# A decoder step with a product-key expert layer: row numbers by exclusive-or and minimum, negated scores, sink column and gate sums on ScalarE

## What is computed

```python
def banded_attention(q, k, v, sink):
    ...
    s = jnp.where(mask[None, :, None, None], s, -jnp.inf)
    lse = jax.nn.logsumexp(s, axis=-1)
    if sink is not None:
        lse = jnp.logaddexp(lse, sink.astype(jnp.float32)[:, :, None])
    p = jnp.exp(s - lse[..., None])
...
        s1, i1 = lax.top_k(sc[:, :, 0], PEER_TOPK)
        s2, i2 = lax.top_k(sc[:, :, 1], PEER_TOPK)
        cand = (s1[..., :, None] + s2[..., None, :]).reshape(...)
        cid = (i1[..., :, None] * N_KEYS + i2[..., None, :]).reshape(...)
        top_s, pos = lax.top_k(cand, PEER_TOPK)
        eid = jnp.take_along_axis(cid, pos, axis=-1)
        gate = jax.nn.softmax(top_s, axis=-1)
        act = jax.nn.gelu(jnp.einsum('cd,chkd->chk', hc, u[eid]))
        return jnp.einsum('chk,chkd->cd', gate * act, v[eid])
```

## Time and profile before

| | |
|---|---|
| median of 3 runs | 3233.87 us (3221.91 to 3236.2) |
| span of the profiled execution | 3236.3 us |
| instructions | 37338 |
| granted TensorE clock, mean | 0.946 |
| moved by all transfers | 1258.27 MB, 389 GB/s in the mean |
| of these, the gathers' queue | 1086.39 MB, 83.0% of 16 engines' span |
| the other transfers' main queue | 169.50 MB, 13.9% |

### The profile page before, as it was taken

How to read it: one execution, slowest core, us unless ns; L and a number is a source line. 1 busy time by engine, 2 the same in 40 slices (tenths; PEclk the granted TensorE clock), 3 DMA queues, 4 the chain that set the end, 5 groups by cost and what they waited for, 6 DMA issues and landing times.

```text
span 3236.3 us, 37338 instructions
## 1 busy us (share of the span) xinstructions
PE 2680.4 (83%) x8698; PEld 1435.6 (44%) x8698; DVE 2511.3 (78%) x5990; ACT 1835.9 (57%) x5839; POOL 1352.4 (42%) x1044
## 2 busy tenths in 40 slices
PE   7768878889997888899899888888788888767776
PEld 4444444445553444555444444443334444334342
DVE  1288868888788998878888887887678888977775
ACT  1246645578544556865555567774455556555554
POOL 0043423354343344433433444542344544556663
PEclk9889989999998998989999999998999999999999
DMA  8999989999999999989999999999999999999997
GB/s 329 353 372 413 382 346 420 394 411 419 398 382 381 406 405 394 409 344 395 403 398 358 405 385 379 415 410 349 356 373 397 403 386 399 393 409 421 421 421 317
DMA packets 189061, 1258.27 MB, mean 389 GB/s; under 512 B 24592, under 2 KB 32616, under 8 KB 44432
## 3 DMA queue, kind: packets, MB, share of 16 engines
q0 software_dynamic: 149760, 1086.39, 83.0%
q1 hardware_dynamic: 39080, 169.50, 13.9%
HBM read 1247.04 MB, written 43.37 MB: 399 GB/s over the span
## 4 chain that ended last, share of the span: by engine, by line
DMA 28%; DVE 24%; PE 23%; ACT 7%; issue 7%; DVEq 4%; SPq 3%; POOL 2%; ACTq 1%; POOLq 0%
DMA uv_ring<-in_peer_uv,idx 24%; PE acc L1787 10%; DVE uv_ring L2482 10%; DVE accs L2489 4%; PE pS L1655 3%; PE pS L1528 3%; POOL uv_ring L1469 2%; ACT bent L2086 2%; PE pA L1678 2%; ACT wv L2089 1%; SPq L1366 1%; SPq L1333 1%; ACT diag L1859 1%; DMA S<-in_cache_swa 1%; PE acc L1528 1%
## 5 line engine op out<-in xcount | busy, mean ns | idle before, releaser
L1469 POOL DMA_INDIRECT uv_ring<-in_peer_uv,idx x1024 | 1336.9, 1306 | 1841.8 <-PE acc L1787 1384.3
L1787 PE MATMUL acc<-uv_ring,diag 128*128 128x512 f32 x2536 | 1291.1, 645 | 373.9 <-ACT diag L1859 373.0
L2482 DVE SCALAR_TENSOR_TENSOR uv_ring<-uv_ring,hb 128x1024 f32<-128x1024 f32 x1032 | 1240.1, 1221 | 316.9 <-DMA uv_ring<-in_peer_uv,idx 292.6
L1787 PEld LDWEIGHTS acc<-uv_ring,diag 128*128 128x128 f32 x2536 | 477.5, 201 | 966.6 <-ACT diag L1859 509.0
L2082 ACT ACTIVATE cube<-dots 128x1 f32<-128x1 f32 x1032 | 205.4, 199 | 849.9 <-DVE uv_ring L2482 844.3
L2489 DVE SCALAR_TENSOR_TENSOR accs<-uv_ring,wv,accs 128x1024 f32<-128x1024 f32 x390 | 499.3, 1280 | 28.9 <-ACT wv L2089 28.1
L2086 ACT ACTIVATE bent<-dots,cube 128x1 f32<-128x1 f32 x1032 | 399.1, 387 | 74.6 <-issue 3.5
L1801 PE MATMUL acc<-maskB,zeros 128*96 128x256 f32 x1600 | 394.2, 386 | 0.0
L1801 PEld LDWEIGHTS acc<-maskB,zeros 128*96 128x96 f32 x1600 | 263.8, 167 | 172.2 <-issue 109.5
L1859 ACT ACTIVATE diag<-diag,wv 128x128 f32<-128x128 f32 x634 | 254.6, 402 | 54.3 <-issue 4.0
L2089 ACT ACTIVATE wv<-bent,dots 128x1 f32<-128x1 f32 x634 | 245.3, 387 | 45.1 <-issue 1.4
(11 more groups left out here) (287 smaller groups left out, 2265.5 us busy)
## 6 DMA issues: line engine op xcount, KB each, us to landing
wbuf<-in_w_q SPq DMA_DIRECT2D x40, 1024.0 KB, 9.7
out_dil_s<-in_cache_dil SPq DMA_DIRECT2D x8, 4092.0 KB
wbuf<-in_w_in SPq DMA_DIRECT2D x26, 1024.0 KB, 9.7
wbuf<-in_w_out SPq DMA_DIRECT2D x20, 1024.0 KB, 9.7
uv_ring<-in_peer_uv,idx POOLq DMA_INDIRECT x1024, 10.8
uv_ring<-in_w_in SPq DMA_DIRECT2D x6, 1024.0 KB, 16.7
keysT<-in_keys SPq DMA_DIRECT2D x40, 128.0 KB, 12.4
T<-in_xT_all SPq DMA_DIRECT2D x8, 512.0 KB, 15.4
```

Source lines behind the costliest of these rows:

```text
L1469: pool.indirect_dma_start(uv_ring[:, entry % RING, :], None, peer_uv, bass.IndirectOffsetOnAxis(rows, 0))\
L1787: m = pe.matmul(acc[0:R, side * 512:(side + 1) * 512], w, uv_ring[:, entry % RING, D + side * 512:D + (side + 1) * 512], start=first, stop ...
L2482: dve.scalar_tensor_tensor(row, row, GELU_C, h, ALU.mult, ALU.mult, accum_out=dots[:, e % RING:e % RING + 1]).then_inc(u_dot, 1)
```

## The change

It has five parts.

- Scores are formed with -0.125 and a minimum, so that the reduction gives the negated maximum at once (`anm`). The sinks are negated once. ACT's exponents take scale -1.
- The sink becomes one more column of the banded scores. ACT copies it there ahead of its wait for the maxima, and the exponent's own sum contains it; the addition on DVE goes.
- The place bits and the key numbers are coded such that the exclusive-or of a wanted rank with an entry is the key number where the ranks agree, and 128 or more where not. A minimum over the 16 entries then gives the number. `places_of` becomes one OR and one shift with AND, and comparison and product become one exclusive-or.
- The subtraction before the gates' exponents goes: ACT makes the negated largest sum by a copy and takes it as a bias. It does so one tile at a time, and takes the sums along (`accum_out`).
- `times_of` has new costs for `sm`, `vd`, `r1`, `r2`, `r3`, `gd` and `ge`.

```diff
-        return (("DVE", {"r2": (2.5, 3.36), "r3": (1.77, 2.58), "gd": (0.75, 0.79)}[kind][tiles - 1]),)
+        return (("DVE", {"r2": (1.25, 1.8), "r3": (0.95, 1.5), "gd": (0.5, 0.52)}[kind][tiles - 1]),)
-        "s": (("PE", 0.64 if first else 0.64 + 0.21 * n),), "sm": (("DVE", 1.12 if first else 1.12 + 0.135 * n),),
+        "s": (("PE", 0.64 if first else 0.64 + 0.21 * n),), "sm": (("DVE", 0.88 if first else 0.88 + 0.135 * n),),
-        "vd": (("DVE", 0.5),), "vo": (("ACT", 0.41),),
+        "vd": (("DVE", 0.27),), "vo": (("ACT", 0.41),),
-        "r0": (("DVE", 3.23),), "r1": (("DVE", 2.75),), "ge": (("ACT", 0.15),),
+        "r0": (("DVE", 3.23),), "r1": (("DVE", 2.48),), "ge": (("ACT", 0.9),),
-        "so": (("DVE", 1.15),), "sr0": (("DVE", 3.2),), "sr1": (("DVE", 2.7),), "sr2": (("DVE", 2.55),), "sr3": (("DVE", 1.74),),
-        "sge": (("ACT", 0.15),), "sgd": (("DVE", 1.08),),
+        "so": (("DVE", 1.15),), "sr0": (("DVE", 3.2),), "sr1": (("DVE", 2.7),), "sr2": (("DVE", 1.3),), "sr3": (("DVE", 0.95),),
+        "sge": (("ACT", 0.6),), "sgd": (("DVE", 0.8),),
...
                 b = par if t == 0 or piped(t) else 0
-                act.wait_ge(a_max, A + 1)
                 n = blocks_of(t) * P
                 B = S[:, 640 * par:640 * par + P] if t == 0 else S[:, 0:n]
-                Aw = S[:, 640 * par + 256:640 * par + 384] if t == 0 else S[:, D:D + 256]
-                act.activation(B, B, ACT.Exp, bias=anm[:, b, 0:1], accum_out=aden[:, b, 0:1])
-                act.activation(Aw, Aw, ACT.Exp, bias=anm[:, b, 1:2], accum_out=aden[:, b, 1:2])
-                act.activation(aden[:, b, 2:3], sink[:, h:h + 1], ACT.Exp, bias=anm[:, b, 1:2]).then_inc(a_exp, 1)
+                Aw = S[:, 640 * par + 256:640 * par + 385] if t == 0 else S[:, D:D + 257]
+                if A == 0:
+                    act.wait_ge(a_max, 1)
+                last = 640 * par + 384 if t == 0 else D + 256
+                copy(S[:, last:last + 1], sink[:, h:h + 1])
+                act.drain()
+                act.wait_ge(a_max, A + 1)
+                act.activation(B, B, ACT.Exp, scale=-1.0, bias=anm[:, b, 0:1], accum_out=aden[:, b, 0:1])
+                act.activation(Aw, Aw, ACT.Exp, scale=-1.0, bias=anm[:, b, 1:2], accum_out=aden[:, b, 1:2]).then_inc(a_exp, 1)
 
...
                 n = len(prompt_of(GROUPS[g]))
-                act.activation(gexp[:, 0:n, :], gsub[:, 0:n, :], ACT.Exp).then_inc(r_exp, 1)
+                copy(gneg[:, 0:n], candv[:, 0:n, 0], -1.0)
+                act.drain()
+                for u in range(n):
+                    m = act.activation(gexp[:, u, :], candv[:, u, :], ACT.Exp, bias=gneg[:, u:u + 1],
+                                       accum_out=gsum[:, u:u + 1])
+                m.then_inc(r_exp, 1)
 
             def sample_gate_exp():
                 act.wait_ge(sr_sub, 1)
-                act.activation(gexp[0:64, 1, :], gsub[0:64, 1, :], ACT.Exp).then_inc(sr_exp, 1)
+                copy(gneg[0:64, 1:2], candv[0:64, 1, 0:1], -1.0)
+                act.drain()
+                act.activation(gexp[0:64, 1, :], candv[0:64, 1, :], ACT.Exp, bias=gneg[0:64, 1:2],
+                               accum_out=gsum[0:64, 1:2]).then_inc(sr_exp, 1)
 
...
                     dve.wait_ge(c2_in, 16 * (9 + NS))
+                    dve.tensor_scalar(sink[:, :], sink[:, :], -1.0, None, ALU.mult)
                 dve.wait_ge(a_s, A + 1)
...
                     dve.tensor_tensor_reduce(S[:, base:base + P], pS[:, 512 * par:512 * par + P], maskB[:, 7 * P:],
-                                             0.125, NEG, ALU.add, ALU.max, amax[:, b, 0:1])
+                                             -0.125, -NEG, ALU.add, ALU.min, anm[:, b, 0:1])
                     dve.tensor_tensor_reduce(S[:, base + 256:base + 384], pS[:, 512 * par + 256:512 * par + 384],
-                                             maskA[:, P:], 0.125, NEG, ALU.add, ALU.max, amax[:, b, 1:2])
+                                             maskA[:, P:], -0.125, -NEG, ALU.add, ALU.min, anm[:, b, 1:2])
                 else:
                     need(dve, a_t, A)
                     n = blocks_of(t) * P
-                    dve.tensor_tensor_reduce(S[:, 0:n], pS[:, 0:n], maskB[:, D - n:], 0.125, NEG, ALU.add, ALU.max,
-                                             amax[:, b, 0:1])
+                    dve.tensor_tensor_reduce(S[:, 0:n], pS[:, 0:n], maskB[:, D - n:], -0.125, -NEG, ALU.add, ALU.min,
+                                             anm[:, b, 0:1])
                     near = pS[:, 768:1024] if piped(t) else pM[:, 0:256]
-                    dve.tensor_tensor_reduce(S[:, D:D + 256], near, maskA[:, :], 0.125, NEG,
-                                             ALU.add, ALU.max, amax[:, b, 1:2])
-                D_()
-                dve.tensor_tensor(amax[:, b, 1:2], amax[:, b, 1:2], sink[:, h:h + 1], ALU.max)
-                D_()
-                dve.tensor_scalar(anm[:, b, :], amax[:, b, :], -1.0, None, ALU.mult).then_inc(a_max, 1)
+                    dve.tensor_tensor_reduce(S[:, D:D + 256], near, maskA[:, :], -0.125, -NEG,
+                                             ALU.add, ALU.min, anm[:, b, 1:2])
+                D_()
+                dve.tensor_tensor(anm[:, b, 1:2], anm[:, b, 1:2], sink[:, h:h + 1], ALU.min).then_inc(a_max, 1)
 
...
                 D_()
-                dve.tensor_tensor(aden[:, b, 1:2], aden[:, b, 1:2], aden[:, b, 2:3], ALU.add)
-                D_()
-                dve.reciprocal(arden[:, b, :], aden[:, b, 0:2]).then_inc(a_rd, 1)
+                dve.reciprocal(arden[:, b, :], aden[:, b, :]).then_inc(a_rd, 1)
 
...
                 dve.tensor_scalar(cand[0:R, 128:136], second[:, 8:16], first[:, 0:1], None, ALU.add)
-                top16([(cand[0:R, :], candv[0:R, u, :], candp[0:R, u, :])])
-                return dve.tensor_scalar(gsub[0:R, u, :], candv[0:R, u, :], candv[0:R, u, 0:1], None, ALU.subtract)
+                return top16([(cand[0:R, :], candv[0:R, u, :], candp[0:R, u, :])])
 
             seen_g = [0]
 
             def numbers_half(half, c, R):
                 n = c.stop - c.start
                 full = [R, n, TOPK, TOPK]
-                hot = onehot[0:R, c, :, :]
-                D_()
-                dve.tensor_tensor(hot, candf[0:R, half, c, :].unsqueeze(3).broadcast_to(full),
-                                  iota[0:R, :].unsqueeze(1).unsqueeze(1).broadcast_to(full), ALU.is_equal)
-                D_()
-                dve.tensor_tensor(hot, hot, topif[0:R, c, half, :].unsqueeze(2).broadcast_to(full), ALU.mult)
-                D_()
-                dve.tensor_reduce(sel[0:R, half, c, :], hot, AX_X, ALU.add)
+                apart = onehot[0:R, c, :, :].bitcast(U32)
+                D_()
+                dve.tensor_tensor(apart, candk[0:R, half, c, :].unsqueeze(3).broadcast_to(full),
+                                  topi[0:R, c, half, :].unsqueeze(2).broadcast_to(full), ALU.bitwise_xor)
+                D_()
+                dve.tensor_reduce(sel[0:R, half, c, :], apart, AX_X, ALU.min)
 
             def places_of(c, R):
 
-                p = candp[0:R, c, :]
-                D_()
-                dve.tensor_copy(topif[0:R, c, :, :], topi[0:R, c, :, :])
-                dve.tensor_scalar(candh[0:R, 0, c, :], p, 3, 15, ALU.logical_shift_right, ALU.bitwise_and)
-                dve.tensor_scalar(candh[0:R, 1, c, :], p, 4, 8, ALU.logical_shift_right, ALU.bitwise_and)
-                D_()
-                dve.tensor_copy(candf[0:R, 0, c, :], candh[0:R, 0, c, :])
-                dve.scalar_tensor_tensor(candh[0:R, 1, c, :], p, 7, candh[0:R, 1, c, :], ALU.bitwise_and, ALU.bitwise_or)
-                D_()
-                dve.tensor_copy(candf[0:R, 1, c, :], candh[0:R, 1, c, :])
+                n = c.stop - c.start
+                D_()
+                dve.tensor_tensor(topi[0:R, c, :, :], topi[0:R, c, :, :],
+                                  codes[0:R, 0:32].rearrange("p (s a) -> p s a", s=2).unsqueeze(1)
+                                  .broadcast_to([R, n, 2, TOPK]), ALU.bitwise_or)
+                dve.scalar_tensor_tensor(candk[0:R, :, c, :], candp[0:R, c, :].unsqueeze(1).broadcast_to([R, 2, n, TOPK]), 7,
+                                         codes[0:R, 32:96].rearrange("p (s u k) -> p s u k", s=2, u=2)[:, :, c, :],
+                                         ALU.logical_shift_left, ALU.bitwise_and)
                 numbers_half(0, c, R)
...
                 n = c.stop - c.start
-                D_()
-                dve.tensor_reduce(gsum[0:R, c], gexp[0:R, c, :], AX_X, ALU.add)
                 D_()
...
     mask_sb = np.concatenate([np.repeat(log_count(1024 - rows[None, :], dil), 64, axis=0), new], axis=1)
+    place = np.arange(16, dtype=np.uint32)
+    codes = np.concatenate([place << 3, (place & 7) | ((place & 8) << 4)])
+    rank_codes = np.concatenate([codes, np.repeat(np.array([0x78, 0x87], np.uint32), 32)]).astype(np.uint32) << np.uint32(7)
```

(31 more changed lines are left out.)

1 line of the change is left out of this document (removed).

## The result

The changed kernel takes 3202.9 us in the median of 4 runs (3196.0 to 3204.8), against 3235.0 before. The ratio is 0.9892 with a 95% interval of 0.9871 to 0.9914: 1.1% faster, some 35 us by the ratio and 32 by the two medians. The forecast was 3192.

The account below looks back on a forecast made before the run. Transfers were taken to bound the picks-only end and, at 0.96 to 0.99 share with DVE behind, nearly the rest. Passed relief 45 plus 4 at the start minus 7 for ACT gives 3233.9 - 42 = 3192 us; range 3165 to 3215, 8-in-10 3145 to 3245.

Parts of the forecast that it names:

- the loss by half speed: Row numbers on DVE: if exclusive-or ran at half speed, it would cost 34 us; no row supported that.
- near 120: DVE over the whole kernel: busy time falls by near 120 us, against 132 us counted start to start.
- 33 us with bounds of 17 and 40: Gate on ACT: 33 us added; 17 if reads and drains overlap wholly, 40 if a drain costs 0.25.
- the exponent with its read: Gate on ACT, once per tile: exponent with bias and accumulator read, taken as 0.48 us.
- the forecast's 20 to 60: Planner: 20 to 60 of PE's 634 weighings move to DVE, spending half of DVE's relief again.
- I therefore let 0.4 of it through, 45 us, 4 at the start, and take off 7: Ranking stages: 0.4 of 112 us returnable relief passes; with start gain and ACT's cost, 42 us saved.
- The signs named for it: After the change: two ranking stages shorter by 10 us or more each at over 400 GB/s, among other signs.
- E and C: Ranking of the last group, and an earlier group's ranking beside attention: gaps of 24 and 37 us at full transfer rate.
- The transfers bound it already: Rival: with transfers at 0.98 share, only the start and a few deep gaps gain, 7 us: 3227; chance 0.20.
- ACT takes the place: Rival: ACT's 33 us between product and gate delay slots, a tenth of DVE's relief passes: 3253 us; chance 0.14.
- All of it passes: Rival: DVE sets the pace wherever near full, so 112 + 6 = 118 us return: 3116 us; chance 0.10.
- F's rate: Last stretch, picks alone: the transfers bound it, with a DMA share of 1.01 at 419 GB/s.

Follow-up runs that it names:

- Experiment 11: Changed kernel with every gather from the eighth on bringing 4 KB per token in place of 8, so it doesn't compute the layer: 2955.6 us.
- experiment 1: Changed kernel's instructions in the old order, by putting only the planner's old costs back: 0.9950 of the kernel before.
- experiment 7: Changed kernel in its own order, with the gates' subtraction and sum put back on DVE: 0.9901 of the kernel before.
- experiment 6: Kernel before with negated scores, sink column and gate sums on ACT, row numbers as before, in the old order: 0.9979 of the kernel before.
- experiment 4: Changed kernel with row numbers computed as before and their old costs, so in an order of its own: 1.0013 of the kernel before.

## Why the prediction held, and where a step was off

**What bounds it.** Right in kind: the transfers at 0.98 of the share with the engines close behind. Experiment 11 puts numbers on it: 2956 us for the engines, an estimated 3003 for the transfers. It was PE rather than DVE that stood nearest, with 87% against 82% there.

**The costs on DVE.** The exclusive-or runs at the comparison's rate; the loss by half speed fell away. The small steps take 0.44 for the 0.40 taken. DVE's busy time fell by 96 us at an equal split (experiment 1), where "near 120" stood: busy time counts overlapping instructions once, not twice as I had it, so removing an overlapped one saves less of it (the durations in DVE's rows of before add up to over 2710 us, where the page counts 2511). In the changed kernel it fell by 68, with 33 us of moved weighings.

**ACT.** Forecast 33 us with bounds of 17 and 40; measured 19 of busy time at an equal split, and all of it in the gate (experiment 7 gives the 19 back). The term that was too large is the exponent with its read: 0.31 us from start to start in the timeline, where 0.48 was taken, since the read overlaps with the exponent before it and with what follows. The rule of the Trainium skill, "ScalarE: Activation LUTs", Rules for kernel authors, to leave plain arithmetic to VectorE is neither borne out nor refuted: putting the gate's sums back (experiment 7) made no difference that can be told. The trace agrees with it in direction only: the negation of 128x2 takes 201 ns on ACT now, and took 183 in the mean on DVE.

**The plan.** 26 weighings moved, within the forecast's 20 to 60, which makes 416 on DVE, over the 410 named. No new gap opened: POOL's longest waits are 17.8 us for PE and 3.6 for DVE's weighing, after 18.1 and 21.7.

**How much comes back.** This is the step that was off inside a sum that came out near: "I therefore let 0.4 of it through, 45 us, 4 at the start, and take off 7". In the order of before all of it together returned 16 us, 0.12 of the relief; the other 19 came when the order was made for the new costs. The signs named for it show the same: E and C were to be shorter at over 400 GB/s. They are shorter by 45 and 78 us, but at 393 and 399. I had treated the plan as a place where relief is spent again; without the new plan less than half of the gain was there. The factor 0.4 had no row behind it, and that 42 us stood near the measured 35 is luck. One premise of it was also misread: POOL waits eight times as long for PE as for DVE, but 527 times against 112, not eight times as often.

**The rivals.** "The transfers bound it already" is what the work alone came near to: 16 us, where 7 was its price, and DVE's wait for rows grew by 98. "ACT takes the place" foresaw a slower kernel. It is refuted by experiment 1, and by experiment 6, where ACT's added work stands beside only 51 us of relief and the kernel is still not slower (0.9961 to 0.9996). Its sign did appear: PE's wait for ACT's diagonal is 401 us in after, 373 before. But it is 431 with the old work in the new order and 407 with the gate off ACT, so it goes with the order and not with ACT's longer gate. "All of it passes" is refuted by experiment 1.

**What stays open.** Three orders made with the new costs for the new work lie at 0.9892, 0.9872 and 0.9860, the old one at 0.9950, and the order's detail is worth about 0.3%. So for the whole change each new order is better than the one old order that was run. By which feature isn't shown, since an order with early base work and one with spread base work both have it. That a plan made for the real costs is better in general isn't shown either: for the change without the numbers it was worse (experiment 4 against 6). And no second order from the old costs was run with the new work, so the old one may be a poor one of its kind for it.

## What to carry to other kernels

When a kernel's order is computed from costs, an edit has two effects, the work and the new order. Time the new work in the old order and the old work in the new one before you credit any part: here the numbers looked like the whole gain and the rest like none, and in a fixed order each was worth some 7 us, with 1 to 13 possible. Know the size of the order's accidents by moving a foreign cost a little; a smaller difference between two kernels in different orders says nothing about their instructions.

Where transfers and engines each need nearly the whole time, and a small ring of slots couples them, relief on one engine can return little (0.12 in one order here, 0.46 in another). A smoother mixture of heavy and light work did as well here as early base work; whether it can do better is open.

## What the runs showed that I had not expected

- A foreign cost moved by 0.03 us in the planner, which shifts 5 weighings to PE and the order of the rest, moved the time by 0.33% (interval 0.14 to 0.53%).
- The engines alone take 2956 us, the transfers at F's rate 3003 us, together 3203. Of the 200 us between, 90 to 145 are left for the coupling once start, end and the slower stage D are looked at, about as much as all relief of this change; that the slots are its cause is argued.
- Beside that, a minimum over uint32 input takes what the sum over float took: 686 ns against 0.69 us over 128x512.
